# A hybrid attention and recurrence layer: attention and levels of the sample frames placed between the jobs of the input projection, and the state products of the sample frames placed after the turn of the normalised output

## What is computed

```python
h = rmsnorm(x, ln1) * (1 + sc1) + sh1
qa, ka, va, qb, fb, ib, gb = jnp.split(jnp.dot(h, w_in), SPLITS, axis=-1)
...
    oa = swa_sample(qa, ka, va, k_cache, v_cache, sinks)      # softmax over 128 cached and 16 new keys and a sink
...
    S, ob = hgrn_block(S0, qh, kb, ih, logf)
ob = rmsnorm(ob, o_norm) * jax.nn.silu(gb)
mix = jnp.concatenate([oa, ob], axis=-1)
x = x + g1 * jnp.dot(mix, w_out)
...
x = x + g2 * moe(h2, w_router, router_bias, w_e_gate, w_e_up, w_e_down)
```

## Time and profile before

| | us |
|---|---|
| median of 3 runs (lowest, highest) | 1375.74 (1369.49, 1376.49) |
| the profiled execution's own time | 1372.43 |
| its span, from the first to the last instruction | 1370.7 |
| busy in the span: PE, PEld | 1212.1 (88%), 1005.8 (73%) |
| busy in the span: DVE, ACT, POOL | 736.7 (54%), 550.0 (40%), 344.7 (25%) |
| first instruction of `sampling`, of `mixing`, from the span's start | 369.33, 437.05 |

### The profile page before, as it was taken

The page is one execution under the profiler, slowest core; times in us unless marked ns, Lnnn a source line. Parts: engine busy times, 40 slices in busy tenths (PEclk is TensorE's granted clock), DMA queues, the critical chain, the costliest instruction groups (busy, mean ns, idle before and its releaser), DMA issues. The chain is left out here.

```text
span 1370.7 us, 21647 instructions
## 1 busy us (share of the span) xinstructions
PE 1212.1 (88%) x7081; PEld 1005.8 (73%) x7082; DVE 736.7 (54%) x1075; ACT 550.0 (40%) x921; POOL 344.7 (25%) x410
## 2 busy tenths in 40 slices
PE   4789999999776999999999627999999999799964
PEld 1567889988655888888888526888887887578853
DVE  1553520352355477766666475664375585556861
ACT  2553421333432345544444204444163464444650
POOL 1000100122422333333332002331432342333322
PEclk9799999999856899999998858999999999989987
DMA  9625771522183433312330193687579889987864
GB/s 352 230 93 173 271 279 69 197 83 70 50 240 81 133 104 104 105 43 93 104 98 24 66 360 100 214 264 239 160 213 369 271 266 331 307 281 250 282 227 92
DMA packets 119430, 249.87 MB, mean 182 GB/s; under 512 B 17713, under 2 KB 47153, under 8 KB 116290
## 3 DMA queue, kind: packets, MB, share of 16 engines
q1 hardware_dynamic: 107266, 204.92, 43.0%
q0 software_dynamic: 12096, 44.05, 12.4%
HBM read 205.02 MB, written 43.93 MB: 182 GB/s over the span
## 5 line engine op out<-in xcount | busy, mean ns | idle before, releaser
L2125 PE MATMUL psum<-e_w_h,e_x_h 128*128 128x512 f32 x432 | 174.7, 404 | 31.0 <-DVE w_gu L2238 24.2
L2127 PE MATMUL psum<-e_w_h,e_x_l 128*128 128x512 f32 x432 | 171.6, 397 | 0.0
L2126 PE MATMUL psum<-w_gu,e_x_h 128*128 x432 | 171.4, 397 | 0.0
L2072 POOL DMA_INDIRECT out<-e_work,e_to x26 | 87.9, 3379 | 302.4 <-DVE e_work L2226 302.4
L2238 DVE TENSOR_TENSOR w_gu<-w_gu,e_w_h 128x1024 f32 x128 | 146.7, 1217 | 21.7 <-ACT e_w_h L2179 21.7
L2179 ACT ACTIVATE e_w_h<-w_gu 128x1024 fp32r x128 | 123.0, 1048 | 55.0 <-issue 33.2
L2125 PEld LDWEIGHTS psum<-e_w_h,e_x_h 128*128 128x128 f32 x432 | 83.3, 193 | 49.4 <-DVE w_gu L2238 24.7
L499 PE MATMUL psum<-p_w_h,p_h_h 128*128 128x512 f32 (+1 forms) x288 | 107.6, 374 | 10.1 <-DVE p_h_l L655 10.1
L500 PE MATMUL psum<-p_w_l,p_h_h 128*128 128x512 f32 (+1 forms) x288 | 106.3, 369 | 0.0
L501 PE MATMUL psum<-p_w_h,p_h_l 128*128 128x512 f32 (+1 forms) x288 | 106.0, 368 | 0.0
L2127 PEld LDWEIGHTS psum<-e_w_h,e_x_l 128*128 128x128 f32 x432 | 83.0, 192 | 18.1
(11 more groups left out here) (382 smaller groups left out, 2586.6 us busy)
## 6 DMA issues: line engine op xcount, KB each, us to landing
w_gu<-in_w_e_gate SPq DMA_DIRECT2D x16, 2048.0 KB, 10.5
w_gu<-in_w_e_up SPq DMA_DIRECT2D x16, 2048.0 KB, 15.4
w_dn<-in_w_e_down SPq DMA_DIRECT2D x16, 2048.0 KB, 15.2
shared<-in_w_ada SPq DMA_DIRECT2D x24, 1024.0 KB, 6.4
p_w_raw<-in_w_in SPq DMA_DIRECT2D x5, 2048.0 KB, 9.2
tok_d<-p_tok SPq DMA_DIRECT2D x27, 256.0 KB, 2.0
feat_d<-p_work SPq DMA_DIRECT2D x12, 576.0 KB, 3.8
p_work<-in_x SPq DMA_DIRECT2D x9, 512.0 KB, 3.9
```

The costliest lines, as they stand in the source:

```text
L2072: pool.indirect_dma_start(out=d["y"], out_offset=bass.IndirectOffsetOnAxis(ap=to_now[1 - par][:, 0:1], axis=0), in_=y_s[:, 1 - par, :], in ...
L2125: pe.matmul(psum[:, j, :], x_h[:, k, :], wh, start=(k == 0), stop=False)
L2126: pe.matmul(psum[:, j, :], x_h[:, k, :], wl, start=False, stop=False)
L2127: last = pe.matmul(psum[:, j, :], x_l[:, k, :], wh, start=False, stop=(k == KC - 1))
```

## The change

The reduction to the sample rows' attention, from the turns of the keys to the normalised attention output `o_a`, and the whole of the levels are taken out of `sampling` and put into `projection`, a step behind each of certain jobs of the groups qa and g on every engine. `JQ` and `JG` are the first jobs of the two groups. The sample tile becomes the first job of qa, so that its queries are there early.

```diff
-JOBS = [(g, n) for g, (name, _, _) in enumerate(GROUPS) for n in range(4 * NCH if name in BY_WEIGHT else NT)]
+JOBS = [(g, (n - 1) % NT if name == "qa" else n) for g, (name, _, _) in enumerate(GROUPS)
+        for n in range(4 * NCH if name in BY_WEIGHT else NT)]
 FIRST_JOB = [next(i for i, job in enumerate(JOBS) if job[0] == g) for g in range(len(GROUPS))]
+JQ, JG = FIRST_JOB[4:6]
+KS = WIN + L
+BP = NB // 2
+FIRST_LEVEL = LEVELS.index(L // 2)
```

SP loads `tok` earlier, and issues the new values and the old states (two loads a job) between the stores of g; the eight sink loads go to the first job of qa:

```diff
-                if name == "g" and i == 2:
-                    wait_tok_stored(FIRST_JOB[g])
...
+                if n == JG + 1:
+                    sp.wait_ge(s["job_done"], JG)
+                    sp.dma_start(v_new[:, :, :], tok_d[tile_cols(TP), TOK_V:TOK].rearrange("(n l) w -> l n w", l=L)).then_inc(s["vnew_loaded"], 16)
+                if n >= JG + 1:
+                    for h in range(2):
+                        sp.dma_start(b["state"][h * HD:(h + 1) * HD, :, n - JG - 1, :],
+                                     state_in[n - JG - 1].rearrange("(c h) k v -> h k c v", h=2)[h]).then_inc(b["state_loaded"], 16)
+                if n == JQ + 3:
+                    wait_tok_stored(JQ + 1)
                     sp.dma_start(tok_s[:, TOK_I:TOK_I + QW], tok_d[tile_cols(TP), TOK_I:TOK_I + QW]).then_inc(b["tok_in"], 16)
```

PE, in its loop over the jobs, behind the matmuls of job n (`level(i)` and `scores(kv)` hold the same 8 and 16 matmuls as before, `scores` now for one key head at a time into the same two banks):

```diff
+                if n == JQ + 2:
+                    pe.wait_ge(b["feat_in"], 16)
+                    pe.wait_ge(s["row_done"], SB + 1)
+                    for h in range(8):
+                        r, c = slice((h % 2) * HD, (h % 2 + 1) * HD), slice((h // 2) * P, (h // 2 + 1) * P)
+                        last = pe.matmul(psum[:, ADA + h % 2, c], kb_s[r, c], qb_s[r, c], start=True, stop=True)
+                        if h >= 6:
+                            last.then_inc(s["diag_mm"], 1)
...
+                    pe.wait_ge(b["cache_loaded"], 16)
+                    pe.wait_ge(s["h_mult"], NT)
+                    for j in range(NB):
+                        last = pe.transpose(psum[:, X0 + j // 4, (j % 4) * P:(j % 4 + 1) * P], cache_k_sb[:, j, :], ident[:, :])
+                    last.then_inc(s["cache_turned"], 1)
...
+                if n == JQ + 5:
+                    pe.wait_ge(b["tok_in"], 2 * 16)
+                    pe.wait_ge(s["cache_t_ready"], 1)
...
+                if n == JQ + 6:
+                    level(0)
+                if n == JQ + 7:
+                    pe.wait_ge(s["qt_ready"], 1)
+                    scores(0)
+                if n == JQ + 8:
+                    level(1)
+                if n == JG:
+                    pe.wait_ge(s["score_kept"], 1)
+                    scores(1)
+                if n == JG + 1:
+                    level(2)
+                if n == JG + 3:
+                    level(3)
+                if n == JG + 4:
+                    pe.wait_ge(s["probs_ready"], 1)
+                    for j in range(8):
...
+                if n == JG + 5:
+                    pe.wait_ge(s["pt_ready"], 1)
...
+                if n == JG + 6:
+                    pe.wait_ge(s["pt_ready"], 2)
+                    pe.wait_ge(b["cachev_loaded"], 16)
+                    pe.wait_ge(s["vnew_loaded"], 16)
...
+                            pe.matmul(o, pc_t[:, j, q], cache_v_sb[:, 2 * bp + par, v], start=True, stop=False)
+                            last = pe.matmul(o, pn_t[:, j, q], v_new[:, 2 * bp + par, v], start=False, stop=True)
+                    last.then_inc(s["pv_mm"], 1)
```

ACT and DVE, behind their eviction of job n (the functions hold the operations that stood in `sampling`, on buffers that are free by then):

```diff
+                if n == JQ + 3:
+                    for j in range(SL):
+                        act.wait_ge(s["gap_ready"], j + 1)
+                        a(gap[:, j, :], gap[:, j, :], ACT.Exp).then_inc(s["gap_exp"], 1)
...
+                if n == JQ + 6:
+                    act.wait_ge(s["qk_turned"], 1)
...
+                if n in (JG + 2, JG + 3):
...
+                if n == JG + 4:
+                    act.wait_ge(s["pc_turned"], 1)
...
+                if n == JG + 5:
+                    act.wait_ge(s["pn_turned"], 1)
```

```diff
+                if n == JQ + 2:
+                    sample_gaps()
+                if n == JQ + 3:
...
+                if n == JQ + 4:
+                    sample_queries()
+                if n == JQ + 5:
+                    penalties()
+                if n == JQ + 7:
+                    place(0)
+                if n == JQ + 8:
+                    keep_scores(0)
+                if n == JG:
+                    place(1)
+                if n == JG + 1:
+                    keep_scores(1)
+                    maxima()
+                if n == JG + 2:
+                    place(2)
+                if n == JG + 4:
+                    place(3)
+                    dve.wait_ge(s["probs_ready"], 1)
...
+                if n == JG + 7:
+                    dve.wait_ge(s["pv_mm"], 1)
```

```diff
+            sp.dma_start(w_raw[:, G:KC, :], d["w_out"][QW:2 * QW, :].rearrange("(c p) n -> p c n", p=P)).then_inc(s["w_b_loaded"], 16)
...
-            link(pool.memset(q_m[:, :, :], 0.0))
...
+            pool.wait_ge(s["qm_clear"], 1)
             pool.wait_ge(s["expb_ready"], 1)
...
+            last.then_inc(s["oa_turned"], 1)
...
-            pe.wait_ge(s["kdt_ready"], 1)
-            pe.wait_ge(s["im_ready"], 1)
-            pe.wait_ge(s["pair_ready"], NL)
-            for h in range(8):
-                last = pe.matmul(psum[(h % 2) * HD:(h % 2 + 1) * HD, M0 + h // 2, :], kd_tok[:, h * HD:(h + 1) * HD],
-                                 i_m[:, h, :, :].rearrange("p n v -> p (n v)"), start=True, stop=True)
-            last.then_inc(s["state_mm"], 1)
...
+            pe.wait_ge(s["kdt_ready"], 1)
+            pe.wait_ge(s["im_ready"], 1)
             pe.wait_ge(s["ob_ready"], 1)
             for c in range(4):
                 last = pe.transpose(psum[:, OUT_B, c * P:(c + 1) * P], o_n[:, c * P:(c + 1) * P], ident[:, :])
             last.then_inc(s["ob_turned"], 1)
+            state_part(range(8)).then_inc(s["state_mm"], 1)
 
...
+            act.wait_ge(s["kd_turned"], 1)
+            a(kd_tok[:, :], psum[:, OUT_B, :], ACT.Copy).then_inc(s["kdt_ready"], 1)
+            act.wait_ge(s["w_b_loaded"], 16)
+            split(range(G, KC))
+            act.wait_ge(s["ob_mm"], 2)
+            act.wait_ge(s["consts"], 1)
+            a(o_sq[:, :, :].rearrange("p (a c) d -> p a (c d)", a=2), psum[:, PJ0:PJ0 + 2, 0:4 * HD], ACT.Square).then_inc(s["osq_ready"], 1)
+            act.wait_ge(s["oss_ready"], 1)
+            inverse_root(o_ss[:, :], o_rs[:, :], HD, Chain(act, s["o_rs"]))
+            act.wait_ge(s["w_a_loaded"], 2 * 16)
+            split(range(G))
             act.wait_ge(s["ob_turned"], 1)
...
+            dve.memset(q_m[:, :, :], 0.0).then_inc(s["qm_clear"], 1)
+            split(range(G, KC), 0)
             dve.wait_ge(s["osq_ready"], 1)
             dve.tensor_reduce(o_ss[:, :], o_sq[:, :, :], AX_X, ALU.add).then_inc(s["oss_ready"], 1)
...
+            split(range(G), G)
+            dve.wait_ge(s["state_mm"], 1)
+            dve.wait_ge(b["state_loaded"], 2 * NB * 16)
+            last = last_bc(by_request(exp_b[:, :])[:, :, L - 1:L], HD)
+            old, new = (ap.rearrange("p c n v -> p (c n) v") for ap in (state[:, :, :, :], new_state))
+            link(dve.tensor_tensor(new, old, last, ALU.mult))
+            dve.tensor_tensor(new, new, psum[:, M0:M0 + 4, :].rearrange("p c (n v) -> p (c n) v", v=HD), ALU.add).then_inc(s["state_ready"], 1)
```

More of the change, by code:

```diff
@@ L349, in _ @@
                 name = GROUPS[g][0]
[L350 removed]
+                if n == FIRST_JOB[g] and g >= 1 and g + 1 < len(GROUPS):
                     load_w(g + 1)
@@ L459, in turn_x, with level, scores @@
                 last.then_inc(s["x_turned"], 1)
+            def level(i):
+                pe.wait_ge(s["lv_ready"], i + 1)
+                if i == 0:
+                    pe.wait_ge(s["pair_clear"], 1)
+                else:
+                    pe.wait_ge(s["pair_ready"], i)
+                for h in range(8):
+                    r = slice((h % 2) * HD, (h % 2 + 1) * HD)
+                    c = h // 2
+                    last = pe.matmul(psum[:, ADA + h % 2, c * HD:(c + 1) * HD], gap[r, i, c * P:(c + 1) * P],
+                                     q_l[r, i, c * HD:(c + 1) * HD], start=True, stop=True)
+                    if h >= 6:
+                        last.then_inc(s["lv_mm"], 1)
+            def scores(kv):
+                r = slice(kv * HD, (kv + 1) * HD)
+                for j in range(NB):
+                    bp, par = j // 2, j % 2
+                    o = psum[par * HD:(par + 1) * HD, X0 + bp // 2, (bp % 2) * 256:(bp % 2) * 256 + KS]
+                    pe.matmul(o[:, 0:WIN], q_t[r, j, :], cache_t[r, j, :], start=True, stop=True)
+                    last = pe.matmul(o[:, WIN:KS], q_t[r, j, :], k_new_t[r, j * L:(j + 1) * L], start=True, stop=True)
+                last.then_inc(s["score_mm"], 1)
             pe.wait_ge(s_const, 1)
@@ new lines, in place @@
+            def place(j):
+                h = LEVELS[FIRST_LEVEL + j]
```

(30 more changed lines are left out.)

396 lines of the change are left out of this document (166 added, 230 removed).

## The result

| | before | after |
|---|---|---|
| ratio of the runs, after to before (95% interval) | | 1.0093 (1.0067 to 1.0118) |
| median, us (lowest to highest, 20 runs each) | 1373.55 (1364.68 to 1392.72) | 1394.33 (1376.9 to 1404.14) |
| profiled execution, us | 1372.43 | 1383.29 |
| its span | 1370.7 | 1381.5 |
| first instruction of `sampling`, of `mixing` | 369.33, 437.05 | 395.56, 445.05 |

The change makes the kernel slower by 0.9%, some 12.8 us. The median lies further off than the ratio because more of the changed kernel's runs fall near 1400 us, and the ratio leaves the highest runs out.

A forecast was written before the change was run, and what follows sets the result against it. PE was taken to bound the projection jobs and a chain of dependent steps the sampling. Adding 19.8 us to the projection, with a 49.2 us block, starts mixing 1.2 us later: 1375.74 + 1.2, about 1377 us, range 1369 to 1387.

The forecast's parts named there:

- rival 2: Projection: the clock falls during the 64 value records; the fall costs 5.0 us, mixing 6.2 us late, 1382; chance 0.23.
- within 0.5%: Whole kernel: a time within 6.9 us either way, called no change; chance 0.64.
- The range: Whole kernel: 1369 to 1387 us, leaving a tenth out at each end.
- What bounds the kernel: PE bounds the qa and g jobs, busy 97.76 of 97.80 us; sampling is bound by a chain of dependent steps.
- The products added to the projection: PE in the projection: diagonals 1.2, scores 2.7, levels 4.4, turns 4.1, value products 7.4; sum 19.8 us, all on the path.
- No cost on ACT, DVE, POOL and SP: Projection: steps added on these engines cost nothing, since a job leaves ACT 3.48 and DVE 1.95 us idle at its start.
- rival 3: Projection: PE waits up to 5 us for a step, DVE's price for the penalties being uncertain; 1382; chance 0.11.
- The block: Sampling, from its start to mixing: 20.4 + 3.5 + 1.1 + 6.3 + 4.7 + 13.2 = 49.2 us, instead of 67.7.
- Rival 1: Sampling: the clock rises during the old-state products, which take 9.7 us; mixing 2.2 us earlier than now, 1373.5; chance 0.17.
- the pause between the blocks: Sampling's start: after this pause the old-state products run at the lower clock, 13.1 us instead of 7.4.
- The moved state products: Sampling: 6.3 us of state products now stand behind a normalisation they had no part in; no saving, new state late.
- From the mixing's start to the end: Mixing and after: a shift of mixing's start, 1.2 us later, counts in full in the kernel's time.

## Where the prediction was right and where it was wrong

It said 1377, no change, in a range of 1369 to 1387. The ratio of 1.0093 is on the side of rival 2, and its interval (from 1.0067) leaves out the "within 0.5%" that was called no change. The range held by little: 12.8 us make 1386.3 from the median of 1373.55 measured beside the change, but 1388.5 from the 1375.74 that the forecast started from, and the median of 1394.33 lies above. That it held is in part luck; what carried it that far is rival 2, which set its upper end. Step by step:

- **What bounds the kernel** held. PE is busy in all of the jobs' 123.40 us, the block is a chain, and a delay put into it came out in the time (9.2 us put in, 9.2 more, give or take 4.6).
- **The products added to the projection** are the step that failed. At the upper clock they sum to 19.3 us, as predicted (19.8); the value products took 8.2 there, and 7.4 was forecast. But the clock did not stay up: 4.1 us, rival 2. And the sum had no term for interrupting the jobs, 0.2 us at each of eleven places, 2.3 us. In all 25.7 instead of 19.8.
- **Rival 2** named the place, the sign and nearly the price (5.0 forecast, 4.1 and 2.8 measured), and had 0.23. It counted half of the fall's length; the value records lose less, 0.20 us each instead of 0.128. The argument against it, that the old-state products held the upper clock for 7.4 us, did not carry over. They hold it behind large products, as the runs with the state products first and with the six extra products show; the value records stand behind a job's large products too, and the clock fell all the same. The two differ in shape and length (64 x 64 and 0.0575 us a record against 64 columns by 128 or 16 rows and 0.128 us); which of it decides is not shown.
- **No cost on ACT, DVE, POOL and SP** held. PE has no idle time in the jobs, so rival 3 did not come.
- **The block** held in nearly each term: `q_m` ready at 7.4 (7.3 forecast), old-state products 13.9 at 0.50 (13.1), 3.6 to the turn (3.5), state products 5.6 (6.3), first store at 36.2 (36), 13.2 from there to the mixing, 49.5 in all (49.2). Rival 1 did not come: 403.1 to 416.9 at 0.50. The reason given for that low clock, the pause between the blocks, is not enough: with the pause filled the old-state products were at 0.50 again, behind their wait for `q_m`.
- **The moved state products** were called late by a norm, and are: their order costs 11.8 us. That the same order also takes the upper clock from the old-state products was not seen, though the earlier trace rows have it: there the state products come first and the old-state products follow at 1.00.
- **From the mixing's start to the end.** The forecast took the rest as unchanged. The mixing is, in the profiles that can be set side by side (351.3 and 351.4); the experts took 2.8 us more in both profiles of the changed kernel, and 577.8 to 584.3 in all in the eleven others, in which nothing of them was touched either, so I give it no cause.
- **The range** rested on three runs that lay 7 us apart. Twenty runs of the kernel before lie 28 us apart. In the changed kernel such a spread goes with the clock; no profile of the kernel before was taken in one of its long runs.

With the mixing's start 8.0 and 9.6 us late in the two profiles of the changed kernel, and 2.8 behind it, the two spans are 10.8 and 12.4 us over the profile before; the measured ratio makes 12.8. What stays open is why so many more of the changed kernel's runs reach 1400.

## What to carry to other kernels

Work moved from an idle stage into a full one costs its own time plus a bit for every interruption, and the moved small products can pull the clock down for the large ones that follow; take them apart, a few behind every few large products, before counting on the upper clock. When a step is put behind another one, look also at what it stood ahead of: here large products were what brought the next step to full speed. And a gain of 5 us at the start of a long stage does not show in a dozen runs if the clock in that stage moves the time by 20.

## What the runs showed of the hardware

- The granted clock fell from 1.00 to 0.50 with PE busy without a pause, in a run of 64-column products between 128x512 ones (at 367.4 in the changed kernel, 372.3 in its second profile, and in all four others with these products on end), and it did not fall in five profiles with the same products in eight pieces. The Trainium skill (TensorE: Matmul & The Clock Gate, "HAM oscillation — how this bites in real kernels") puts a lost clock down to PE's waits for data; here there was none.
- One set of products, 128 records of 64 columns, took 13.92 us behind small products and 2.2 or 4.3 us of idle time, and 7.36 us behind 128x512 products (in the kernel before with 2.0 us of pair products between), in each of the profiles.
- In the mixing, where its pieces stand as before, a first fall of 10.2 us that is followed by another in the next tile repeats in three or four tiles on end, 44.3 us apart, 13.7 us long; where the next tile escapes, the falls stay single. By windows of 0.1 us the first fall began 18.94 and 19.04 us behind the fourth load of `x` in the two profiles of the changed kernel, without repeating, and 19.11 to 19.17 us in four others, all of which repeat; behind the fifth load it is 18.80 and 18.89 us without, 18.95 with; behind the sixth, once, 18.78 without. Less than a tenth of a microsecond goes with 20 us of the run; what sets it is open.
